# A two-block transformer on one core: one row of even attentions, a filling piece kept, an advance step of its own

## What is computed

```python
# even layer
o_a = dense_causal_attention(q, k, v_a)            # 8 heads, "mla"
o_b = dilated_mixture(qd, kd, qkv[:, :, 2])        # 3 groups x 4 heads, "dil"
o = jnp.concatenate([o_a, o_b], axis=-1); y = o @ w_out
...
# odd layer
o_c = diff_causal_attention(qc, kc, vc, lam)       # 4 heads, two maps each, p[0] - lam * p[1]
o_c = rms_norm(o_c, diff_subln) * (1.0 - lam_init)
o_d = moba_attention(qm, km, m[:, :, 2])           # 8 heads
o = jnp.concatenate([o_c, o_d], axis=-1); y = o @ w_out
```

## Time and profile before

| what | us |
|---|---|
| median of 3 runs | 1329.57 |
| lowest and highest | 1328.1, 1330.85 |
| profiled execution | 1330.73 |
| its span | 1328.9 |
| TensorE busy in the span | 1283.7 |
| VectorE, ScalarE, GpSimd busy | 912.8, 659.3, 110.9 |

### The profile page before, as it was taken

The page is one execution under the profiler, slowest core; times in us unless marked ns, Lnnn a source line. Parts: engine busy times, 40 slices in busy tenths (PEclk is TensorE's granted clock), DMA queues, the critical chain, the costliest instruction groups (busy, mean ns, idle before and its releaser), DMA issues.

```text
span 1328.9 us, 15849 instructions
## 1 busy us (share of the span) xinstructions
PE 1283.7 (97%) x6336; PEld 1059.7 (80%) x6336; DVE 912.8 (69%) x1223; ACT 659.3 (50%) x888; POOL 110.9 (8%) x145
## 2 busy tenths in 40 slices
PE   8999999999999999999999989999999979999998
PEld 6878888887887888888799877888887867888886
DVE  6968777766686777775768847857667785644444
ACT  6645433443563543444475546544446663644542
POOL 2002000001000100000225200000004320000000
PEclk9999999999999999999999999999999998999999
DMA  9625678773642678886264305876755421455450
GB/s 377 243 69 221 239 306 307 306 281 131 216 157 97 225 272 306 306 307 230 66 210 145 109 1 207 308 294 265 286 222 190 159 96 64 159 190 185 167 187 32
DMA packets 41113, 270.35 MB, mean 203 GB/s; under 512 B 4656, under 2 KB 4672, under 8 KB 12880
## 3 DMA queue, kind: packets, MB, share of 16 engines
q1 hardware_dynamic: 38288, 259.83, 52.9%
q0 software_dynamic: 2464, 8.98, 1.9%
q10 hardware_dynamic: 288, 0.52, 0.1%
HBM read 268.27 MB, written 1.05 MB: 203 GB/s over the span
## 4 chain that ended last, share of the span: by engine, by line
PE 81%; DVE 9%; ACT 5%; issue 2%; POOL 1%; DMA 0%; ACTq 0%; DVEq 0%; POOLq 0%
PE ps L1602 49%; PE ps L1592 25%; PE ps L1616 4%; DVE WB L1924 2%; PE ps L1704 2%; ACT WB L1717 2%; ACT E L1717 1%; PE ps L1679 1%; DVE st L2140 1%; ACT XTH L1717 1%; DVE SCR L2042 1%; POOL st L1514 1%; DMA GB<-xTd 0%; DVE SCR L2043 0%; DVE st L2293 0%
## 5 line engine op out<-in xcount | busy, mean ns | idle before, releaser
L1924 DVE TENSOR_TENSOR WB<-RAW,WB 128x2048 fp32r<-128x2048 f32 (+3 forms) x211 | 453.2, 2151 | 241.1 <-ACT WB L1717 240.9
L1717 ACT ACTIVATE WB<-RAW 128x2048 fp32r<-128x2048 f32 (+3 forms) x211 | 379.9, 1803 | 220.4 <-PE ps L1602 216.4
L1592 PE MATMUL ps<-WB,XTH 128*128 128x512 f32 (+3 forms) x1176 | 313.0, 387 | 12.8 <-ACT XTH L1717 7.7
L1602 PE MATMUL ps<-WB,XTH 128*128 128x512 f32 (+3 forms) x1176 | 306.0, 381 | 7.4 <-DVE WB L1924 7.3
L1602 PE MATMUL ps<-WB,XTL 128*128 128x512 f32 (+3 forms) x1176 | 303.5, 379 | 1.0 <-DVE XTL L1997 0.5
L1602 PEld LDWEIGHTS ps<-WB,XTH 128*128 128x128 f32 x1176 | 218.1, 189 | 50.7 <-DVE WB L1924 12.3
L1592 PEld LDWEIGHTS ps<-WB,XTH 128*128 128x128 f32 x1176 | 213.2, 189 | 52.8 <-ACT XTH L1717 12.6
L1602 PEld LDWEIGHTS ps<-WB,XTL 128*128 128x128 f32 x1176 | 218.0, 188 | 40.4 <-DVE XTL L1997 1.3
L1592 PE MATMUL ps<-WB,HTH 128*128 128x512 f32 (+1 forms) x452 | 126.9, 396 | 0.6 <-ACT HTH L1717 0.5
L1602 PE MATMUL ps<-WB,HTH 128*128 128x512 f32 (+1 forms) x452 | 126.5, 395 | 0.0
L1602 PE MATMUL ps<-WB,HTL 128*128 128x512 f32 (+1 forms) x452 | 126.4, 394 | 0.0
(11 more groups left out here) (183 smaller groups left out, 948.8 us busy)
## 6 DMA issues: line engine op xcount, KB each, us to landing
RAW<-W SPq DMA_DIRECT2D x220, 1024.0 KB, 4.9
RAW<-W SPq DMA_DIRECT2D x22, 768.0 KB, 4.4
VEC<-vecd POOLq DMA_DIRECT2D x10, 512.0 KB, 7.8
RAW<-W SPq DMA_DIRECT2D x8, 512.0 KB, 3.9
RAW<-W SPq DMA_DIRECT2D x4, 576.0 KB, 3.8
RAW<-W SPq DMA_DIRECT2D x2, 648.0 KB, 3.9
T<-sgwd POOLq DMA_DIRECT2D x2, 512.0 KB, 8.5
X<-xd SPq DMA_DIRECT2D x1, 1024.0 KB, 18.5
```

The source lines that it names most:

```text
L1592: eng.matmul(banks[b][:, 0:cw], x2[j][0], hi[:, j, c0:c0 + cw], start=first and j == 0, stop=False)
L1602: op = eng.matmul(banks[b][:, 0:cw], x2[j][0 if low_w else 1], (lo if low_w else hi)[:, j, c0:c0 + cw], start=False, stop=last and end and ...
L1717: return eng.activation(dst, src, f, **k)
L1924: eng.tensor_tensor(WB[:, it["raw"], 0:w], RAW[:, it["raw"], 0:w], WB[:, it["high"], 0:w].bitcast(F32), ALU.subtract).then_inc(*up("wl", n))
```

## The change

`linear_k` yields once more, after `advance()`, so that the high and the loads that it issues have a step of their own. The filler counts follow: in the first block step 2 takes two steps, so that the advance falls in step 2 and everything behind it where it was.

In the even layer the mla and dil units form one list of 14 with one call of `attention`; the old filler, three steps of the projection, the gain and the rest of the projection are chained. Step 5 (the last mla unit) now also takes the advance and the first turn of MIX, step 7 the first matmuls of the projection, step 8 the gain. From step 9 on it is as before.

In the odd layer the first attention takes only three filler steps. The fourth piece (222) and the advance are issued in step 0 of the second attention, which has low steps (`soon`) from 0 on. The copies of E of the diff units are named (`by`): ACT for three, DVE for the last; since `alt()` is not called for them, the moba units' copies shift from act, dve, act, act, dve, act to act, act, dve, act, act, dve.

```diff
--- before.py
+++ after.py
@@ -1,3 +1,4 @@
+import itertools
 import math
 from contextlib import ExitStack
 
@@ -417,6 +418,7 @@
             assert len(its) <= cur["pairs"]
             g, ps, left = uid(), [None, None], [len(its), len(its)]
             advance()
+            yield
             for a, t, *mm_ in steps:
                 if not mm_:
                     turn_rows(a, t)
@@ -643,7 +645,8 @@
             def turns(u, pad):
                 i = u["i"]
                 u["t"] = turn([E[:, i, c:c + 128] for c in u["blocks"]], [u["x"]] + p_free[i],
-                              lambda a, c: PET[:, i, a * 128:(a + c) * 128].rearrange("p (n q) -> p n q", n=c), 128, pad)
+                              lambda a, c: PET[:, i, a * 128:(a + c) * 128].rearrange("p (n q) -> p n q", n=c), 128, pad,
+                              u.get("by", ()))
                 e_free[i] = [u["t"][-1]]
 
             def values(u):
@@ -935,7 +938,7 @@
 
             fill = chain(gating(), linear_k("w_o", mo, put_o(0), turn_o, ((4, 0), (4, 0, 0), (0, 0), (0, 0, 0), (4, 1, 0),
                                                                           (0, 1), (0, 1, 0))))
-            attention(units, fill, (1, 1, 1, 1, 2, 1, 1, 0), first=1, pads=(0, 2, 2))
+            attention(units, fill, (1, 1, 2, 1, 2, 1, 1, 0), first=1, pads=(0, 2, 2))
             run(fill)
             t_pe = [keys_[1]["op"]]
             sel_free = [keys_[1]["op"]]
@@ -1185,7 +1188,7 @@
 
                 def turn_groups(t):
                     tw2[t] += turn_T([H[:, t, n * 128:n * 128 + 128] for n in range(12)],
-                                     qkr[t] + [("score", (mla[5]["id"], 0))], 0, t, by=("act", "act", "act") if t else ("dve", "act", "dve"))
+                                     qkr[t] + [("score", (units[5]["id"], 0))], 0, t, by=("act", "act", "act") if t else ("dve", "act", "dve"))
                     tw2[1] += tw2[0] if t else []
 
                 turn_heads(0, 0, 1)
@@ -1199,7 +1202,6 @@
                     [ch[3, 1][1]], None])
                 SMm = [col(8), col(8)]
                 keys_, units = [], []
-                mla = units
                 for t in range(2):
                     nk = 128 * (t + 1)
                     ok = {}
@@ -1216,12 +1218,10 @@
                                           roots=(RQ[t][:, a:a + per].unsqueeze(1), ("mla", 0, t)),
                                           sums=[SMm[t][:, h:h + 1] for h in hh], outs=outs,
                                           blocks=[c * 128 for c in range(per * (t + 1))]))
-                attention(units, fill, (4, 3, 2, 2, 2, 0, 0, 0), ahead={0: [lambda: turn_heads(1, 0)]},
-                          between={0: [lambda: turn_heads(1, 1)], 5: [lambda: turn_groups(0)], 6: [lambda: turn_groups(1)]},
-                          flush=(0, 1, 2), soon=(5,))
-                run(fill)
-                units, between = [], {}
-                steps, flush, soon = (1, 1, 1, 1, 0, 0, 1, 1, 0, 0), (), (0, 1, 2, 3, 4, 5)
+                ahead = {0: [lambda: turn_heads(1, 0)]}
+                between = {0: [lambda: turn_heads(1, 1)], 5: [lambda: turn_groups(0)], 6: [lambda: turn_groups(1)]}
+                steps = (4, 3, 2, 2, 2, 2, 0, 1, 1, 1, 0, 0, 1, 1, 0, 0)
+                flush, soon = (0, 1, 2), (5, 6, 7, 8, 9, 10, 11)
                 SMd = [col(4), col(4)]
                 n_out, nm_out = 6, "even_w_out_2"
             else:
@@ -1292,15 +1292,14 @@
                         s4 = S8[t][:, 2 * a:2 * a + 4]
                         outs = [(h * 128, 128, [(n_ * (t + 1) + kb, H[:, kb, 1024 + h * 128:1152 + h * 128])
                                                 for kb in range(t + 1)]) for n_, h in enumerate((a, a + 1))]
-                        units.append(dict(banks=bks, joint=False, diff=True, same=True, after=tw[t], vafter=dw[2],
+                        units.append(dict(banks=bks, joint=False, diff=True, same=True, by=("dve",) if t and a else ("act",), after=tw[t], vafter=dw[2],
                                           roots=(RQ[0, t][:, 2 * a:2 * a + 4].rearrange("p (n m) -> p m n", m=2), ("odd", 0, t)),
                                           s4=s4, nk=nk, sums=[s4[:, j:j + 1] for j in range(4)], outs=outs, ok=ok,
                                           blocks=[c * 128 for c in range(2 * (t + 1))]))
-                attention(units, fill, (1, 1, 1, 1, 0, 0), ahead=ahead, between=rotated, flush=(0, 1))
-                run(fill)
+                attention(units, fill, (1, 1, 1, 0, 0, 0), ahead=ahead, between=rotated, flush=(0, 1))
                 SMd = [col(8), col(8)]
-                units, between = [], {0: [lambda: normed.pop(0)()], 1: [lambda: normed.pop(0)()]}
-                steps, flush, soon = (0, 1, 2, 1, 1, 1, 0, 0), (), (1, 2, 3, 4)
+                units, ahead, between = [], {}, {0: [lambda: normed.pop(0)()], 1: [lambda: normed.pop(0)()]}
+                steps, flush, soon = (2, 1, 2, 1, 1, 1, 0, 0), (), (0, 1, 2, 3, 4)
                 n_out, nm_out = 8, "odd_w_out_2"
             xg, xo_w = [[], []], [[], []]
 
@@ -1320,9 +1319,10 @@
                     gain(0, 0)
                     yield
 
-                fill = chain(gain_0(), proj((0, 0), (0, 0, 0), (0, 1), (4, 0), (4, 0, 0), (0, 1, 0), (4, 1), (4, 1, 0)))
+                out_ = proj((0, 0), (0, 0, 0), (0, 1), (4, 0), (4, 0, 0), (0, 1, 0), (4, 1), (4, 1, 0))
+                fill = chain(fill, itertools.islice(out_, 3), gain_0(), out_)
             else:
-                fill = proj((0, 0), (0, 0, 0), (0, 1), (0, 1, 0), (4, 0), (4, 0, 0), (4, 1), (4, 1, 0))
+                fill = chain(fill, proj((0, 0), (0, 0, 0), (0, 1), (0, 1, 0), (4, 0), (4, 0, 0), (4, 1), (4, 1, 0)))
             for t in range(2):
                 nk = 128 * (t + 1)
                 ok = {}
@@ -1358,7 +1358,7 @@
                                           roots=(RQ[3, t][:, 2 * a:2 * a + 2 * per].rearrange("p (n m) -> p m n", m=2), ("odd", 3, t)),
                                           ok=ok, vafter=dw[5], sums=[SMd[t][:, h:h + 1] for h in hh],
                                           outs=outs, blocks=[c * 128 for c in range(2 * per * (t + 1))]))
-            attention(units, fill, steps, (), 0, {}, between, flush, soon)
+            attention(units, fill, steps, (), 0, ahead, between, flush, soon)
             t_pe = [keys_[3]["op"]]
             run(fill)
             x_o = x_w
```

## The result

The changed kernel takes 1332.23 us (median of 20 runs, 1330.25 to 1334.64) against 1329.37 us (20 runs, 1327.77 to 1332.35) of the kernel before on the same chip: a ratio of 1.0021, 95% interval 1.0015 to 1.0027. It is 2.9 us slower; the forecast was 1330.0. The profiled execution of after, with 1330.74 us and a span of 1328.9, equals that of before to 0.01 us and is the fourth quickest of the twenty. So the waits are read in the profile, but the size of the loss is not.

A forecast was written before the change was run, and what follows sets the result against it. TensorE, busy 97% of the span, was taken to bound the kernel, so its waits and clock count. First block +2.0, even layer -3.0 and odd layer +1.4 gave +0.4 us: 1330.0 us on the median, range 1325.8 to 1333.4.

The forecast's parts named there:

- First block: Both layers: low ahead of normalise delays TensorE's turn of MIX, loss 1.0 us each; +2.0 us in all.
- Even layer: One row of units: new waits 1.0 and 1.05 us, later 2.15 us wait and low stretch go; -3.0 us.
- the bound of -1.3: Even layer: the term's least gain, -1.3 us, if a low stretch comes again.
- Odd layer: Last piece kept: 6.3 us idle before last diff turn, 2.4 us wait before second unit's turn; +1.4 us.
- The working at full clock: Odd seam, step by step without low clock: 256-key scores at 1103.0 us, where they stood at 1102.80.
- the clock term: Odd layer: the 6.3 us idle must lower the clock; 1.2 us added over what is lost today.
- the two causes named in the working: Odd layer, VectorE: kept piece's low leads before the 6.3 us idle; two lows precede second unit's maxima, wait 2.4.
- The sum: Whole kernel: +2.0 - 3.0 + 1.4 = +0.4 us, on the median 1330.0 us.
- The forecast case: Whole kernel: same time within 0.2%, 2.7 us, as parts cancel; chance 0.60.
- The range: Whole kernel: 1325.8 to 1333.4 us.
- (c): Slower by the clock: even layer's two waits +1.5, odd piece +1.6; sum +3.5, 1333.1 us; chance 0.18.
- The rule weighed in the prediction: Even layer: only a long unbroken idle gap throttles, so two waits of 1 us cost nothing more; trace speaks against.

The follow-up runs named there:

- experiment 1: Only the first block's part of the change, even and odd seams as in the kernel before: 1334.62 against 1330.11 us, ratio 1.0030.
- experiment 2: Only the even layer's part of the change (one row of units), edited against the kernel before: 1327.42 us, ratio 0.9981.
- experiment 4: Edit against experiment 1: the early high's low comes behind normalise on VectorE: 1328.48 us, ratio 0.9987 to the kernel before.
- experiment 7: Edits of experiment 4 and experiment 2 together, odd layer as in the kernel before: 1326.29 us, ratio 0.9962 to the kernel before.
- experiment 12: Repeat of experiment 1 on another chip: 1334.06 against 1330.21 us of the kernel before, ratio 1.0027.
- experiment 3: Only the odd layer's part of the change, with its diff copies, edited against the kernel before: 1333.30 us, ratio 1.0019.
- experiment 9: Whole change with the edit of experiment 4 (first block's low behind normalise): 1328.88 against 1330.98 us of the kernel before, ratio 0.9985.
- experiment 5: Edit against experiment 3: kept piece's low behind the last diff unit's maxima: 1330.25 against 1330.69 us of the kernel before, ratio 0.9996.
- experiment 6: Edit against experiment 3: one high and low issued before the last diff unit's values: 1331.38 us, ratio 1.0007 to the kernel before.
- experiment 11: Edit against experiment 10: odd layer's second unit's scores ahead of the kept piece on TensorE: 1327.15 us, ratio 0.9967 to the kernel before.
- experiment 10: Whole change with the edits of experiment 4, experiment 5 and experiment 6: 1324.86 us, ratio 0.9953 to the kernel before.

## Why the prediction was right and where it was not

**First block: mechanism right, size short.** Forecast +1.0 a layer; the turns of MIX moved by +1.10 and +1.09 against the start of the same layer's scores (62.80 to 82.41 for 62.34 to 80.85 in layer 0, 384.34 to 403.91 for 383.90 to 402.38 in layer 1). At equal clock the part costs 1.9 for the 2.0 forecast. The term was mis-sized by what it left out, the clock, which it put at nothing without a reason: the part alone measures +3.6 to +4.0 by its ratios and +3.2 in the table, of which 1.3 goes with 0.0019 less mean clock. Where those low stretches lie isn't settled: one profile of this part has 6.8 us more of them than before, between 9 and 14 us and in the odd seam, the other has 10 us fewer (the end of the span left out). That the waits bring them about is an inference from run averages, not shown.

**Even layer: right, in its steps too.** Waits of 1.06 and 0.97 for 1.0 and 1.05; the 256-key scores 2.8 us earlier against the transposes ahead of the seam (18.91 us from 754.92 to 773.83 in after, for 21.73 from 753.36 to 775.09 in before), forecast 3.0. The low stretch went, as said; the bound of -1.3 did not come.

**Odd layer: steps right, clock underpriced.** Idle 6.23 for 6.3; wait 2.45 for 2.4, and 2.85 to 2.92 in the other three profiles with this part unmended; the whole seam +1.40 in the first profile for +1.4. That agreement to a tenth is luck of one pair of profiles. The old seam takes 28.29 us in before and 29.86, 29.75, 28.94, 26.72 and 26.71 in experiments 1, 2, 4, 7 and 12, where it is unchanged: 28.4 in the mean. The new one takes 29.69 and 31.07 us in the two profiles of after and 30.63 and 30.08 in experiments 3 and 9: 30.4 in the mean. So it is 2.0 us longer, and eleven runs of the part alone have +2.5. The working at full clock gives 28.5 us for it (1074.5 to 1103.0); the four seams are 1.9 over that, where the clock term was 1.2. The excess lies in two places: from the end of the idle to the second unit's turn they take 16.2 to 16.9 us for 15.6, and from that turn to the 256-key scores 6.6 to 6.9 us for 5.6 in three of the four, each with a low stretch on the matmuls of w_out. In the first profile that second place has none (5.5 us). Experiments 5 and 6 show the two causes named in the working, a low ahead of the maxima each time: the idle falls from 6.22 to 4.02, the wait from 2.92 to 1.60. In experiment 6 the high moves with the low, so there it is the rows of VectorE and ScalarE, and not the edit alone, that name the low.

**The sum.** +0.4 was forecast and +2.9 was measured. By the mean spans of the table the first block's part cost 3.2 us for 2.0, the odd part 2.3 for 1.4, and the even part gave 2.8 for 3.0. These are the 2.3 us by which the parts' sum of 2.7 misses the forecast, and half of them are the first block's. The column "at equal clock" can't be laid beside these terms one by one, because the even term counted the vanished low stretch as a gain and the odd term held 1.2 us for the clock. The forecast case, within 0.2%, was missed narrowly: 2.9 us is 0.21%, and the interval spans 0.15% to 0.27%. The range held. The rival nearest to the outcome is (c), slower by the clock, 1333.1, and it is right in half of its places: the even waits brought no low stretch in any profile, and the first block, where (c) puts nothing, lost most beyond its term. In the odd layer a second low stretch came in three of four profiles, though behind the kept piece and not under it.

**The clock after waits.** After the even layer's waits of 1.06 and 0.97 us the window from 752.00 to 773.83 ran at 1.00; from 1120 to 1125 the clock was 0.66 again, with waits of 0.16 and 1.02 us and none longer since 1103, and all fourteen profiles have a low stretch there, between 1114 and 1130; in the 6.23 us idle it had fallen 1.8 us after the idle began in the first profile, and 4.1 us after in the second. The rule weighed in the prediction (the Trainium skill, TensorE: Matmul & The Clock Gate, section HAM oscillation: it is a long idle gap that throttles) agrees with the even layer, where it did better than I gave it credit for, and with the low level in the long idle; it does not account for the stretch at 1120.

## What to carry to other kernels

When a copy is moved a step earlier, follow what is done with its result by the next engine in order: in the first block and twice in the odd layer the price was a low of 2.3 us ahead of something short for which TensorE waited, and moving those three (one of them with its high) turned +2.8 into -6.2 us. Then look again at what leads: in experiments 6 and 11 the next in line was a high on ScalarE. Do not take one profiled execution's total as the size of a change below 0.3%: the two profiles of the changed kernel differ by 2.8 us, 2.7 of it by half-speed stretches. The same holds for one seam: the old odd seam scatters by 3.2 us over six profiles. Read the waits from the profile and the size from many runs, with the mean clock beside it.

## What was unexpected

- The half-speed stretches in these profiles are 3.4, 6.8 or 10.2 us long (summed from windows of 1 us; in experiment 2 once 17.1), but for a shorter one at the very end of the span. By estimate one of 3.4 us costs up to 1.7 us where it lies on matmuls, half of its length, and nothing where TensorE idles anyway; the one near 335 us cost 1.3.
- They move from one execution of the same kernel to the next: the one between 335 and 340 us in the profile of before is there in the second profile of after and missing in the first, although TensorE waits 2.1 us just ahead in each of them (for the low of a weight piece). The kernel before itself ran with mean clocks from 0.990 (11 runs, mean span 1330.3 us) to 0.996 (8 runs, 1326.1 us).
- The start of layer 0's scores scatters from 62.34 to 62.97 us in twelve of the fourteen profiles, with and without the first block's edit (62.93 in experiment 6, which doesn't have it). Before and after differ there by 0.46 us, and ScalarE's second copy of the input, which waits for its transfer, starts at 7.30 in the one and 7.76 in the other: half a microsecond that belongs to no edit. In the profiles of experiments 9 and 10 the scores start at 64.10 and 64.38 us, and these two alone have a low stretch of 3.4 us between 20 and 25 us.
